# Adaptive norm's product in plain fp32, in the four column groups of the array, in one bank held over eight weight rows

## What is computed

```python
def adaln(cond, w, b):
    m = (jax.nn.silu(cond) @ w + b)[:, None, :]        # (2, 1024) @ (1024, 6144)
    return jnp.split(m, N_MOD, axis=-1)
shift1, scale1, gate1, shift2, scale2, gate2 = mods
h = rmsnorm(x, lp['norm1_g']) * (1.0 + scale1) + shift1
u = h @ lp['w_in']
...
x = x + gate1 * mix
h2 = rmsnorm(x, lp['norm2_g']) * (1.0 + scale2) + shift2
```

## Time and profile before

| | |
|---|---|
| median of 3 runs | 1171.96 us (1171.92 to 1174.23) |
| the profiled execution | 1171.46 us, its span 1169.6 us |
| busy in the span | PE 96%, DVE 88%, ACT 68%, POOL 21% |
| PE busy, 60 to 80 us | 20.00 us |
| PE busy, 150 to 252 us | 101.33 of 102 us |
| PE busy, 252 to 286 us | 28.38 of 34 us |

### The profile page before, as it was taken

One profiled execution on the slowest core, in us unless ns is written; L12 is line 12 of the kernel. 1 busy time (PEld: TensorE's weight loads), 2 busy tenths in 40 slices (PEclk: granted clock), 3 DMA queues, 4 the chain that ended last, 5 costly groups with the idle time before them and its releaser, 6 DMA issues.

```text
span 1169.6 us, 16801 instructions
## 1 busy us (share of the span) xinstructions
PE 1123.5 (96%) x5641; PEld 918.5 (79%) x5641; DVE 1031.2 (88%) x1379; ACT 800.5 (68%) x997; POOL 242.4 (21%) x184
## 2 busy tenths in 40 slices
PE   4999999998998999989999999999999999999996
PEld 1799999874557898668888888888888888888862
DVE  4759999989997465879999999999999999999977
ACT  6553232677874642738888888888888888888842
POOL 1000000001114001123432323323233323232210
PEclk9999999999999999999999999999999999999999
DMA  9673456645547237968999999999899999999995
GB/s 346 192 186 105 124 170 162 166 146 154 171 145 210 83 105 269 361 232 328 381 372 372 373 373 374 368 360 354 349 351 359 366 358 375 365 371 373 359 409 202
DMA packets 123035, 328.06 MB, mean 280 GB/s; under 512 B 28280, under 2 KB 69847, under 8 KB 98151
## 3 DMA queue, kind: packets, MB, share of 16 engines
q1 hardware_dynamic: 98368, 289.34, 67.7%
q0 software_dynamic: 21648, 33.80, 8.5%
q10 hardware_dynamic: 2968, 4.26, 1.0%
HBM read 326.66 MB, written 41.66 MB: 315 GB/s over the span
## 4 chain that ended last, share of the span: by engine, by line
PE 88%; DVE 5%; DMA 3%; ACT 3%; issue 1%; SPq 0%; POOLq 0%; DVEq 0%; ACTq 0%
PE bank L1766 23%; PE bank L1768 23%; PE bank L1767 22%; PE bank L1776 8%; PE bank L1961 2%; PE bank L1949 1%; PE bank L2103 1%; PE bank L1782 1%; DMA raw<-in_mod_w_dram 1%; PE bank L1783 1%; DVE lo L1198 1%; DMA xg<-h_d,ixt 1%; ACT hi L820 1%; PE bank L2222 1%; DMA raw<-in_exp_w_down_dram 1%
## 5 line engine op out<-in xcount | busy, mean ns | idle before, releaser
L1470 DVE TENSOR_TENSOR lgu<-raw,hgu 128x2048 fp32r<-128x2048 f32 x128 | 292.0, 2282 | 2.7 <-ACT hgu L1076 2.7
L1076 ACT ACTIVATE hgu<-raw 128x2048 fp32r<-128x2048 f32 x128 | 245.4, 1918 | 0.0
L1766 PE MATMUL bank<-hgu,xgh 128*128 128x512 f32 x512 | 206.5, 403 | 0.4 <-DVE xgl L1605 0.3
L1768 PE MATMUL bank<-hgu,xgl 128*128 128x512 f32 x512 | 200.9, 392 | 0.0
L1767 PE MATMUL bank<-lgu,xgh 128*128 128x512 f32 x512 | 199.5, 390 | 0.0
L1599 DVE TENSOR_TENSOR lo<-raw,hi 128x2048 fp32r<-128x2048 f32 x64 | 147.9, 2311 | 25.0 <-ACT hi L1085 19.1
L1198 DVE TENSOR_TENSOR lo<-raw,hi 128x2048 fp32r<-128x2048 f32 (+2 forms) x57 | 125.7, 2209 | 29.4 <-ACT hi L820 29.4
L778 POOL DMA_INDIRECT xg<-h_d,ixt x64 | 66.3, 1036 | 388.5 <-DVE gsl L1572 366.5
L787 POOL DMA_INDIRECT y_d<-ys,ixt x62 | 132.3, 2133 | 48.3 <-ACT ys L1118 28.6
L1296 DVE SCALAR_TENSOR_TENSOR zb<-zb,cwt 128x400 f32<-128x400 f32 x240 | 135.6, 633 | 0.6
L1085 ACT ACTIVATE hi<-raw 128x2048 fp32r<-128x2048 f32 x64 | 122.9, 1921 | 4.9 <-DMA raw<-in_exp_w_down_dram 4.9
(11 more groups left out here) (315 smaller groups left out, 2076.5 us busy)
## 6 DMA issues: line engine op xcount, KB each, us to landing
raw<-in_exp_w_gate_dram SPq DMA_DIRECT2D x64, 1024.0 KB
raw<-in_exp_w_up_dram SPq DMA_DIRECT2D x64, 1024.0 KB
raw<-in_exp_w_down_dram SPq DMA_DIRECT2D x64, 1024.0 KB
raw<-in_mod_w_dram SPq DMA_DIRECT2D x20, 1024.0 KB, 5.2
raw<-in_w_in_dram SPq DMA_DIRECT2D x16, 512.0 KB, 5.5
raw<-in_w_in_dram SPq DMA_DIRECT2D x8, 1024.0 KB, 5.3
mraw<-in_mod_w_dram SPq DMA_DIRECT2D x4, 1024.0 KB, 15.8
raw<-in_w_o_attn_dram SPq DMA_DIRECT2D x4, 1024.0 KB, 4.9
```

Source lines behind the costliest of these rows:

```text
L1076: act.activation(hgu[k % 2][:, :, w, :], src, ACT.Copy).then_inc(ghi_done, 1)
L1470: dve.tensor_tensor(lgu[k % 2][:, :, w, :], src, hgu[k % 2][:, :, w, :].bitcast(F32), ALU.subtract).then_inc(glo_done, 1)
L1766: pe.matmul(out, ah, bh, start=first, stop=False)
L1768: return pe.matmul(out, al, bh, start=False, stop=last)
```

## The change

The weights of the adaptive norm are no longer split. An item is now `("mod", s, k)`: 128 rows (block k) by 2048 columns (third s), loaded as it lies, 8 KB per partition. `mod_item` runs four plain fp32 matmuls of 512 columns on it straight from the landed tile, one for each column block j, with 32 stationary columns (both vectors' block k, repeated with what follows them in `silc`) into partitions 32 j to 32 j + 31: the four column groups of the array. Eight items accumulate into one bank. There are still 24 items of 1 MB, 8 at the start and one per head.

`cst`, `pick`, and the splits of `mod` items on ACT and DVE go away; splits are now counted by `cut_no`. The ring is released by `mod_used`, which PE counts. ACT copies a whole bank (128 x 512) once per third. At the start four transposes replace `column_part`, the bias comes in as columns with the other small rows (`vrow`), and DVE adds it (four more operations, one fewer). The hi splits of `lat` 0,0 and 0,1 stay ahead of the loop on ACT; the lo splits move into and behind the loop on DVE. In attention the modulation bank is held for eight heads, and the other groups rotate over seven banks. POOL issues 8 accumulating transfers.

```diff
 def front_items():
-    it = [("mod", b, h) for b in range(4) for h in range(2)]
+    it = [("mod", 0, k) for k in range(KD)]
...
-    it += [("mod", b, h) for b in range(4, 12) for h in range(2)]
+    it += [("mod", s, k) for s in (1, 2) for k in range(KD)]
...
+    held = len(front) % 8
+    others, at = [(held + 1 + i) % 8 for i in range(7)], 0
+    for g in attention:
+        if g[0] == "mod":
+            take(g, held)
+        else:
+            take(g, others[at % 7])
+            at += 1
...
-                if i >= 12:
-                    sp.wait_ge(lo_done, i - NRAW + 1)
-                elif i >= 8:
-                    sp.wait_ge(lo_done, i - 7)
+                if i >= 8:
+                    held = i - NRAW if i >= 12 else i - 8
+                    if items[held][0] == "mod":
+                        _, s, k = items[held]
+                        if k == KD - 1:
+                            got(sp, ("mod", s))
+                        else:
+                            sp.wait_ge(mod_used, (KD - 1) * s + k + 1)
+                    else:
+                        sp.wait_ge(lo_done, cut_no[held] + 1)
...
+                    sp.dma_start(tile[:, :], mod_w[0, P * k:P * k + P, IW * s:IW * s + IW]).then_inc(landed, 16)
...
             for h in range(H + 4):
-                if h < H - 1:
-                    split(item_no[("mod", 4, 0)] + h + 2)
-                if h < H and h % 2 == 1:
-                    mod_rows(4 + h // 2, modr2[mod_block(h // 2)])
+                if h == H - 2:
+                    split(item_no[("wo", 0)])
+                if h in (KD - 1, H - 1):
+                    mod_rows(1 + h // KD, modr2[:, 512 * (h // KD):512 * (h // KD) + 512])
...
-            for i in range(2, 10):
-                split(i)
...
+            for v in (1, 0):
+                for cc in range(2):
+                    dve.tensor_tensor(abv[:, 1 - v, cc, :].rearrange("p (b k) -> p b k", b=2), pv[:, 2 * v:2 * v + 2, :, 1 - cc],
+                                      vt[:, V_MB + 8 * v:V_MB + 8 * v + 8].rearrange("p (b k) -> p b k", b=2),
+                                      ALU.add).then_inc(ab1_done, 1)
...
+                if k == 1:
+                    split(item_no[("lat", 0, 0)])
...
+            split(item_no[("lat", 0, 1)])
...
-            def mod_half(p, b, h):
-                wh, wl = item(("mod", b, h))
-                for k in range(4):
-                    c4 = cst[:, 4 * (4 * h + k):4 * (4 * h + k) + 4]
-                    pe.matmul(p[0:4, :], c4, wh[:, k, :], start=(h == 0 and k == 0), stop=False)
-                    ins = pe.matmul(p[0:4, :], c4, wl[:, k, :], start=False, stop=(h == 1 and k == 3))
+            def mod_item(p, s, k):
+
+                i = item_no[("mod", s, k)]
+                tile, landed, count = raw_of(i)
+                pe.wait_ge(landed, count)
+                for j in range(4):
+                    ins = pe.matmul(p[32 * j:32 * j + 32, :], silc[:, 2 * k:2 * k + 32], tile[:, 512 * j:512 * j + 512],
+                                    start=(k == 0), stop=(k == KD - 1))
```

More of the change, by code:

```diff
@@ L95, in psum_groups @@
 def psum_groups():
[L97 to L98 removed]
+    g = [("ct",), ("mod", 0), ("vt",), ("cw",), None, ("hT", 0), None, ("hT", 1), ("hT", 2), None, ("modc",)]
+    g += [("lat", 0, 0), ("lat", 0, 1), ("hT", 3), ("lat", 0, 2)]
     g += [("hT", c) for c in range(4, KD)] + [("lat", 1, t) for t in range(NT)]
@@ L109, in psum_groups @@
     g += [("qT", h) for h in range(H)]
+    front = g
+    g = []
     for h in range(H + 3):
-        mod = [("mod", 4 + h // 2)] if h < H and h % 2 == 0 else []
-        scores = [("s", h, t) for t in range(NT)] if h < H else []
-        g += scores + mod if h == 2 else mod + scores
+        if h < H and h % KD == 0:
+            g += [("mod", 1 + h // KD)]
+        if h < H:
+            g += [("s", h, t) for t in range(NT)]
         if h >= 3 and h % 2 == 1:
@@ L124, in psum_groups, with psum_use, take @@
     g += [("list", 1), ("shT", 1), ("shT", 2)]
-    return g
+    return front, attention, g
+def psum_use():
+    use, of_bank = {}, [[] for _ in range(8)]
+    def take(g, b):
+        if g is not None:
+            use[g] = (b, len(of_bank[b]))
+            of_bank[b].append(g)
+    front, attention, back = psum_groups()
+    for i, g in enumerate(front):
+        take(g, i % 8)
+    held = len(front) % 8
[6 more added lines that the diff above has]
+            at += 1
+    for i, g in enumerate(back):
+        take(g, (held + i) % 8)
+    return use, of_bank
 def matmul_order():
[L130 to L133, removed]
+    front, attention, back = psum_groups()
+    g = [n for n in front if n is not None] + attention + back[:back.index(("h2T", 0, 0))]
     g += [("h2T", 0, 0), ("h2T", 0, 1), ("rt", 0), ("shgu", 0), ("h2T", 1, 0), ("h2T", 1, 1)]
@@ L147, in hybrid_step @@
     NI = len(items)
-    groups = psum_groups()
-    use = {n: (i % 8, i // 8) for i, n in enumerate(groups)}
-    assert len(use) == len(groups)
+    cuts = [i for i, n in enumerate(items) if n[0] != "mod"]
+    cut_no = {i: q for q, i in enumerate(cuts)}
+    NC = len(cuts)
+    use, of_bank = psum_use()
     with ExitStack() as ctx:
@@ L421, in read_by @@
             }[k]()
-        halves = [n for n in items if n[0] in ("mod", "lat", "wout") and n[-1] == 0]
+        halves = [n for n in items if n[0] in ("lat", "wout") and n[-1] == 0]
         def wait_used(eng, i):
@@ L1792, in _ @@
             end(("ct",), turn(p[:, 0:16], crow[:, :]))
-            def column_part(b):
-                pe.wait_ge(mod_done, b + 1)
-                for k4 in range(4):
-                    q = 4 * b + k4
-                    ins = pe.matmul(columns[:, 2 * q:2 * q + 2], modr1[0:5, P * q:P * q + P], cst_of("pick", 5),
-                                    start=True, stop=True)
-                return ins
             def turn_hidden_rows(k):
@@ L1835, in _ @@
                 turn_hidden_rows(k)
-            p = begin(("mod", 3))
-            mod_half(p, 3, 0)
-            column_part(2)
-            mod_half(p, 3, 1)
-            end(("modc",), column_part(3))
+            for k in range(6, KD):
+                mod_item(pmod, 0, k)
+            pe.wait_ge(con_in, 16)
+            pe.wait_ge(mod_done, 1)
+            p = begin(("modc",))
+            for k in range(4):
+                ins = turn(p[:, P * k:P * k + P], modr1[:, P * k:P * k + P])
+            end(("modc",), ins)
             first = [begin(("lat", 0, 0)), begin(("lat", 0, 1))]
```

167 lines of the change are left out of this document (61 added, 106 removed).

## The result

The changed kernel takes 1152.59 us (median of 4 runs, 1151.21 to 1156.12), the kernel before 1172.78 beside it: a ratio of 0.9831, 95% interval 0.9806 to 0.9856. It is faster by 20 us, where the prediction said 6.5. Its profiled execution took 1151.21 us, with a span of 1149.4, 20.2 us less than before's.

The account below looks back on a forecast made before the run. PE was taken to bound most of the kernel, with data landing plus about 10 us in the opening and DVE in the first heads; 1171.5 - 2.65 (opening) - 3.6 (attention) = 1165.2, said as 1165; range 1146 to 1195 us.

Parts of the forecast that it names:

- my case: Whole kernel: weight row on PE costs 1.7 to 2.3 us, total 1158 to 1169 us; chance 0.40.
- the rival of full overlap: Weight rows on PE: four column groups run fully at once, 0.86 us a row, total 1146.5 us; chance 0.18.
- x: Price of one weight row of 2048 columns on PE, opening and attention: taken as 2.16 us.
- Its bounds, 0.86 and 3.45: Weight row on PE: 0.86 us if four groups overlap fully, 3.45 us if eight records run in turn.
- 15x - 38.7: Whole kernel: total change in us by weight-row price, opening plus attention; zero at 2.58 us.
- 14x - 33.8: Attention: change in us by weight-row price; -3.6 us at the assumed 2.16 us.
- overlap, but eaten: Heads: draining between 32-column and full-width weights plus waits, about 2.5 us a row, total -1 to +3 us; chance 0.10.
- The late heads: Attention heads 3 to 14: PE sets them, weight row + 4.08 us plus 0.15 us wait, 6.39 us each.
- The opening: Opening and lat block: first ftmp at 36.8 instead of 42.5, -5.7, less +3.1 for splits: -2.65 us.
- +3.1: Lat block in the opening: two DVE splits now inside and behind the loop feeding PE cost 3.1 us.
- a clock that PE's sparser opening keeps low: Opening: named risk, at half clock lat rows take some 3 us instead of 1.71 each; not in the sum.
- the covers costed at nothing: Attention: ACT's whole-bank copies, raw ring, POOL's transfers, SP's loads and wo loads taken as hidden, 0 us.

Follow-up runs that it names:

- Run 10: Changed kernel with each head's weight-row products moved behind the score products, ahead of the values: 1149.1 us, ratio 0.9779 to the kernel before.
- after: The changed kernel itself, without further edits: 1152.59 us, ratio 0.9831 to the kernel before.
- run 7: Changed kernel with each weight row's 1 MB moved by four transfers of 2 KB rows instead of one of 8 KB rows: 1153.58 us, ratio 0.9834.
- run 6: Changed kernel with DVE's second lat split made right behind the fourth hTl instead of behind the loop: 1147.57 us, ratio 0.976.
- best: Changed kernel with the second lat split earlier and the end of attention rearranged (wo splits, conv taps): 1146.65 us, ratio 0.9772.
- best_warm: best plus five unread products on PE ahead of the lat block: 1143.38 us, ratio 0.9739.
- after_again: The changed kernel, unedited, run once more: 1151.49 us, ratio 0.9827.
- run 4: Changed kernel with DVE's subtraction of a 128x2048 tile alone put back in heads 0 to 13, result unused: 1169.22 us, ratio 0.9965.
- run 5: Changed kernel with ACT's copy of a 128x2048 tile alone put back in heads 0 to 13, result unused: 1153.02 us, ratio 0.983.
- warm: Changed kernel with five unread products on PE ahead of the lat block: 1147.76 us, ratio 0.9772.
- act_back: Same as run 5: changed kernel with ACT's 128x2048 copy put back in heads 0 to 13: 1153.02 us, ratio 0.983.
- narrow_rows: Same as run 7: changed kernel with weight rows loaded by four transfers of 2 KB rows: 1153.58 us, ratio 0.9834.
- lat_early: Same as run 6: changed kernel with DVE's second lat split made inside the loop, behind the fourth hTl: 1147.57 us, ratio 0.976.
- scores_first: Same as Run 10: changed kernel with the weight row's products behind each head's scores: 1149.1 us, ratio 0.9779.

## Why the prediction was right and wrong

**Right in direction, 12.5 us short in size** (1165 forecast, 1152.6 measured; inside the range of 1146 to 1195, outside my case's own 1158 to 1169, and nearest to the rival of full overlap, 1146.5, to which I gave 0.18).

**The step that failed is x.** The prediction took 2.16 us because records keep program order and "both passes of one group must follow each other", so that only neighbouring passes could overlap. Measured: 1.00 in four groups, 1.84 in two, 3.55 in one. Its bounds, 0.86 and 3.45, held to 0.1 us: 3.55 is the price of one group, and 1.00 is nearly a quarter. Only the order within was wrong. In the timeline four records run side by side and the other four behind them, so the passes of different groups do not wait in one line. The pairs of records from which I argued all belong to full-width weights or to one group, which share the same columns; they could not show what separate groups do. From one row type I generalized a rule to a case that differed in just the point that mattered.

The Trainium skill, "TensorE: Matmul & The Clock Gate", "Part 3: Packing small matmuls", says that groups of columns run concurrently, with 2.38x for three. Measured here is 3.55x for four plain fp32 groups and 1.93x for two. Of its two statements the speed, which I used only in a sentence beside, was the better guide; its rule that matmuls start and end in order is what I feared would prevent it for two-pass matmuls, and did not.

**The formula 15x - 38.7.** At x = 1.00 it gives -23.7; measured -20.2 by the spans. Its attention part, 14x - 33.8 = -19.8, comes out almost as measured (-18.9 and -0.7), but by two errors that cancel. The opening missed by 2.05 us, and 1.3 came back behind the start of `wo`.
- *The scores' price.* Forecast 1.51, measured 1.71 behind a weight row. It is the mechanism of the rival "overlap, but eaten", which I had set aside because 4-column weights ahead of the scores cost nothing. Run 10 shows that it exists, at 0.2 us a head instead of the some 1.5 that the rival needed. The Trainium skill, "TensorEngine Tiling (Array Packing)", section "Key Properties", says that a change of tiling mode drains TensorE; the runs agree from 32-column groups to full width (0.2 us) and show no such price from 32 to 64 columns.
- *The late heads.* At x = 1.00 the forecast's parts and its 0.15 us of leftover wait make 5.23 us; measured is (324.34 - 259.43) / 12 = 5.41, the scores' 0.20 more: twelve heads, +2.1.
- *The early heads.* Forecast 3.83 us for heads 0 and 1, set by DVE, and 3.42 for head 2 at x = 1.00, 11.1 in all. After's starts 2.7 us apart show that PE runs ahead and DVE catches up while transposes and values are not yet due: 259.43 - 250.48 = 8.95, -2.1.
- *The opening.* First `ftmp` forecast at 36.8, measured 33.91: x is smaller, and the weight rows landed sooner than 32.4 (PE was done with the last at 31.8), which run 7 traces in part to the 8 KB rows. These two are not told apart, and in the seven traces of this opening `ftmp` itself lies between 33.66 and 34.77. But the block then took 23.35 us where the forecast had 19.5. The splits in the loop, "+3.1", were the right mechanism: without the late second one the block is 4.2 us shorter (run 6). The size was off, because the sum set 19.5 us with every row at full clock against before's 16.5, whose own first row had run at 0.28 us a record (44.75 to 48.21, 3.5 us instead of 1.7). What the sum lacked is the clock, which the prediction named at its end without a price in the sum: "a clock that PE's sparser opening keeps low". With the split alone mended the block takes 19.2 us (best), with the clock too 16.9 (best_warm). Of the 6.8 us by which it grew in after, about 2.3 are thus clock alone, and 4.2 the split together with what the clock adds to it. Opening in total: forecast -2.65, measured -1.8 in after and -3.3 in after_again.

**Right:** DVE's subtraction as the 2.20 us that lift a head to 6.03 (run 4), and DVE without it as no limit of the late heads; ACT's split as no loss and no gain by itself once scores don't stand behind it (run 5); PE as the engine that sets the late heads; the covers costed at nothing, since the chain from head 0 to `wo` holds no transfer and no copy of the bank.

**Open.** In what order the unit takes up the passes of the four groups, beyond the two bundles seen; and why warm's total gained more than its chain up to `wo` (339.34 against 339.97). The 1.3 us given back are likely scatter: from the start of its last product of `hgu` and `xgh` (1121.3, 1099.9 and 1098.4 us) to the end before takes 48.3 us, after 49.5, and after_again, the same program, 48.5; from the start of `wo` to the end it is 808.5 to 812.0 us in the traces of after, after_again, act_back, narrow_rows, lat_early, warm and scores_first.

## What to carry to other kernels

When small-output products go to separate column groups of the array, price them as one group's passes, not as a queue, and test the two ends by a kernel with all blocks in one group: it is a change of one index. Put such a bundle where the next product is not full width: moved behind the scores it cost 0.2 us a head less, for free. And where a change empties an engine ahead of a dense block, look whether it ran at half clock before, add to the sum what it costs so, and look for a producer that used to be early and now stands inside the block: here the opening gained 8.6 us at its first product and kept 1.8.

## What the hardware showed that I had not expected

- Four plain fp32 products of 512 columns, each into its own 32-partition part of one bank, take 1.00 us together; in one part 3.55, in two 1.84.
- Full-width weights behind 32-column groups: 1.71 us instead of 1.51 for the next six records, whatever the number of groups used; 64-column weights behind them: 1.44, unchanged.
- TensorE ran at its lower clock (0.28 us for 336 columns instead of 0.155) after a stretch in which it waited for most of the time between the last weight row and the first `lat` product; with five products put into that stretch the granted clock stayed at 1.00. After the wait inside the block it fell again in six of seven traces of this opening, after among them, and in after_again, the same program, it did not: the end of the block differed by 1.5 us.
- While 1 MB items were loaded, from 20 to 30 us, the DMA engines moved 402 GB/s at a share of 1.00 where their rows were 8 KB wide, and 386 at 1.05 where they were 2 KB.
